# Six channel-wise projections of the state-space layer: eight block products each against seven, with weight sums on GpSimd

## The reference

```python
def ssd_dilated_layer(x, norm_w, w_in, conv_w, conv_b, ...):
    h = rms_norm(x, norm_w)
    proj = jnp.einsum("bsd,df->bsf", h, w_in.astype(h.dtype))
    z, xbc, dt, q, k, v, g = split_cols(proj, EVEN_IN_SIZES)
    xbc = jax.nn.silu(causal_dwconv(xbc, conv_w, conv_b))
    xs, bm, cm = split_cols(xbc, (SSD_D_INNER, SSD_GROUPS * SSD_D_STATE, SSD_GROUPS * SSD_D_STATE))
    ...
    y = ssd_chunked_scan(xs, dt, A, bm..., cm...)
    y = y + d_skip * xs
    y = y.reshape(Bsz, S, SSD_D_INNER) * jax.nn.silu(z)
    ...
```

## Time and profile before

| | |
|---|---|
| median of three runs | 1670.7 us |
| span of the profiled execution | 1666.9 us |
| from that span to the median | 3.8 us |
| TensorE busy | 1564.8 us (94%) |
| VectorE busy | 486.1 us (29%) |
| ScalarE busy | 267.3 us (16%) |
| GpSimd busy | 73.5 us (4%) |
| HBM read | 500.43 MB |

### The profile page before, as it was taken

One profiled execution on the slowest core, in us unless ns is written; L12 is line 12 of the kernel. 1 busy time (PEld: TensorE's weight loads), 2 busy tenths in 40 slices (PEclk: granted clock), 3 DMA queues, 4 the chain that ended last, 5 costly groups with the idle time before them and its releaser, 6 DMA issues. The chain is left out here.

```text
span 1666.9 us, 25063 instructions
## 1 busy us (share of the span) xinstructions
PE 1564.8 (94%) x10674; PEld 1038.9 (62%) x10674; DVE 486.1 (29%) x932; ACT 267.3 (16%) x667; POOL 73.5 (4%) x138
## 2 busy tenths in 40 slices
PE   9999999998989899999999998898999899999998
PEld 8855555555555576465556555554888678758874
DVE  4941000000000313440000000002436897346642
ACT  1020000000000112210000000001132233321331
POOL 0000000000000000000000000000000432001220
PEclk9999999999999899999999999999999999999999
DMA  9689999999999942499999999999233224233420
GB/s 389 268 320 370 429 426 429 427 428 428 428 428 427 398 151 101 181 420 412 428 428 428 429 428 428 428 427 423 109 131 122 102 102 151 102 116 137 152 101 26
DMA packets 38519, 502.52 MB, mean 301 GB/s; under 512 B 4272, under 2 KB 4528, under 8 KB 6064
## 3 DMA queue, kind: packets, MB, share of 16 engines
q1 hardware_dynamic: 37872, 499.40, 72.8%
q0 software_dynamic: 576, 2.10, 0.3%
HBM read 500.43 MB, written 1.05 MB: 301 GB/s over the span
## 5 line engine op out<-in xcount | busy, mean ns | idle before, releaser
L854 PE MATMUL ps<-x_tok,tables_sb 128*128 128x256 f32 x1228 | 305.1, 392 | 0.0
L854 PEld LDWEIGHTS ps<-x_tok,tables_sb 128*128 128x128 f32 x1228 | 220.9, 189 | 102.8 <-issue 77.1
L877 PE MATMUL ps<-ring,arena 128*32 128x256 f32 x3968 | 238.6, 382 | 30.2 <-DMA ring<-in_expert_up 20.5
L877 PEld LDWEIGHTS ps<-ring,arena 128*32 128x32 f32 x3968 | 118.5, 109 | 139.2 <-issue 31.0
L719 PE MATMUL ps<-spare,ring 128*128 128x256 f32 x768 | 169.7, 383 | 0.9 <-DVE spare L2121 0.9
L2357 DVE TENSOR_TENSOR arena<-arena,ps 128x128 f32<-128x128 f32 x64 | 18.4, 288 | 497.0 <-ACT arena L1723 497.0
L719 PEld LDWEIGHTS ps<-spare,ring 128*128 128x128 f32 x768 | 147.3, 192 | 22.3 <-DVE spare L2121 1.2
L940 PE MATMUL ps<-ring,arena 128*32 128x512 f32 x928 | 115.0, 612 | 16.4 <-ACT arena L1718 11.3
L1303 PE MATMUL ps<-ring 128*128 128x256 f32 x480 | 110.5, 383 | 1.4 <-ACT tables_sb L1851 1.3
L751 PE MATMUL ps<-ring,arena 128*128 128x512 f32 x224 | 98.7, 595 | 2.9 <-ACT arena L1841 1.3
L1303 PEld LDWEIGHTS ps<-ring 128*128 128x128 f32 x480 | 89.5, 190 | 18.7 <-issue 6.9
(11 more groups left out here) (299 smaller groups left out, 1396.3 us busy)
## 6 DMA issues: line engine op xcount, KB each, us to landing
ring<-in_expert_up SPq DMA_DIRECT2D x124, 2048.0 KB, 20.4
ring<-in_stream SPq DMA_DIRECT2D x43, 2048.0 KB, 8.2
ring<-in_expert_down SPq DMA_DIRECT2D x42, 2048.0 KB, 24.1
ring<-in_expert_down SPq DMA_DIRECT2D x32, 1024.0 KB, 22.3
arena<-in_expert_up SPq DMA_DIRECT2D x4, 2048.0 KB, 11.2
arena<-in_expert_down SPq DMA_DIRECT2D x2, 2048.0 KB, 12.4
tables_sb<-in_expert_down SPq DMA_DIRECT2D x2, 2048.0 KB, 9.9
spare<-in_expert_down SPq DMA_DIRECT2D x2, 2048.0 KB, 10.2
```

The source lines that it names most:

```text
L854: pe.matmul(ps[:, b, 0:TOK], ident, x[:, 0, 0:TOK], start=True, stop=True, skip_group_check=True)
L877: ins = pe.matmul(ps[q * SLOTS:(q + 1) * SLOTS, 4 + e % 2, 0:TOK] .rearrange("p (g n) -> p g n", g=2), xg[:, 4 * half + k, e * SLOTS:(e + ...
```

## The change

The six channel-wise chunks are made by seven products too.

- PE: `seven_channels` issues for each chunk seven products of two channel blocks by four row blocks, with a 128x128 block of the weight (or of t1 to t4) as the stationary operand and 128 tokens (or a sum of token halves) as the moving one: 56 matmuls, 112 records for a chunk.
- GpSimd: `channel_sums` makes the 24 weight sums of these chunks, 128x1024 each, ahead of the first `rotate`. A chunk's sums wait for its arrival, the first ten also for the last chunks of MOE1, later ones for a free place among the ten.
- ScalarE: `keep` copies three partial results of a chunk out of PSUM. The copies into the padded buffer are gone; the last taps read that buffer, and stand behind the first `keep` of the next chunk. The 16 SiLU are in two groups with a `keep` between, and those of `z` read SBUF.
- VectorE: `channel_corner`, `channel_front` and `channel_crossed` put the quarters together in the padded buffer or in `ss_z`: five additions for a chunk, ahead of the taps. For chunks 4 and 5 they stand in the loop that moves the turned blocks.

The diff, cut to its core:

```diff
-    sevens = [base[stage] + n for stage, which in ((SSD, range(6, 15)), (MOBA, (0, 1, 2, 4, 5, 6)))
+    sevens = [base[stage] + n for stage, which in ((SSD, range(15)), (MOBA, (0, 1, 2, 4, 5, 6)))
               if stage in on for n in which]
+    by_channel = 6 if SSD in on else 0
...
+            if is_channel(g):
+                return 4 + 2 * ((g - base[SSD]) % 2)
...
+        def channel_rows(g):
+            c = g - base[SSD]
+            return ss_pad[:, c % 2, :, 3:3 + TOK] if c < 4 else ss_z[:, 4 * c - 16:4 * c - 12, :]
...
+            def channel_sums():
+                for n in range(4 * by_channel):
+                    c, q = divmod(n, 4)
+                    w = slot8[slot(sevens[c])]
+                    if q == 0:
+                        arrive(pool, sevens[c])
+                    if MOE1 in on and n in (0, 4, 8):
+                        pool.wait_ge(chunk_done, base[SSD] - 2 + n // 4)
+                    if n >= W_SUMS:
+                        c6, q6 = divmod(n - W_SUMS, 4)
+                        if q6 == 3:
+                            pool.wait_ge(chunk_done, sevens[c6] + 1)
+                        else:
+                            pool.wait_ge(sem("product"), 6 * c6 + FREED_AT[q6])
+                    if q in (1, 3):
+                        pool.wait_ge(sem("channel_sums"), n if q == 1 else n - 1)
+                    w11, w12, w21, w22 = (w[:, 4 * a_:4 * a_ + 4, TOK * b_:TOK * b_ + TOK]
+                                          for a_ in range(2) for b_ in range(2))
+                    a_, b_ = ((w12, w11), (w22, w_sum[(n - 1) % W_SUMS]), (w22, w12),
+                              (w21, w_sum[(n - 2) % W_SUMS]))[q]
+                    pool.tensor_tensor(w_sum[n % W_SUMS], a_, b_, ALU.subtract)\
+                        .then_inc(sem("channel_sums"), 1)
...
                 if stage == SSD:
+                    channel_sums()
                     if first < SSD:
                         pool.wait_ge(sem("late_in"), 16 * ((first == CONV) + (first < STICK) + 1))
                     rotate(0, gains)
...
+            def seven_channels(g):
+                c, b, w = seven_no[g], seven_bank(g), slot8[slot(g)]
+                low, high, left, right = slice(0, 4), slice(4, 8), slice(0, TOK), slice(TOK, 512)
+                x1, x2 = xT[:, :, 0:P], xT[:, :, P:TOK]
+                t1, t2, t3, t4 = (w_sum[(4 * c + q) % W_SUMS] for q in range(4))
+                products = (
+                    (b, 0, w[:, low, left], x1[:, low], True),
+                    (b + 1, TOK, t1, x_sum[0], True),
+                    (b, 0, t2, x_sum[1], False),
+                    (b + 1, TOK, w[:, high, right], x_sum[2], False),
+                    (b + 1, 0, t3, x_sum[3], True),
+                    (b, TOK, w[:, high, left], x1[:, high], True),
+                    (b + 1, 0, t4, x2[:, high], False))
+                if c >= 2:
+                    pe.wait_ge(sem("ss_proj"), c - 1)
+                arrive(pe, g)
+                for n, (o_b, at, w_, x_, opens) in enumerate(products):
+                    if 0 < n < 5:
+                        pe.wait_ge(sem("added"), n)
+                    if n in (2, 3, 5):
+                        pe.wait_ge(sem("kept"), 3 * c + (2, 3, 5).index(n) + 1)
+                    if n in (1, 2, 4, 6):
+                        pe.wait_ge(sem("channel_sums"), 4 * c + (1, 2, 4, 6).index(n) + 1)
+                    if n == 6:
+                        pe.wait_ge(sem("added"), added_no(g))
+                    for m in range(2):
+                        for k in range(4):
+                            ins = pe.matmul(ps[:, o_b, at + m * P:at + (m + 1) * P],
+                                            w_[:, k, m * P:(m + 1) * P], x_[:, k, :],
+                                            start=(opens and m == 0 and k == 0), stop=(k == 3),
+                                            skip_group_check=True)
+                    ins.then_inc(chunk_done if n == 6 else sem("product"), 1)
...
-                channels(g, 4)
-                channels(g + 1, 6)
+                seven_channels(g)
+                seven_channels(g + 1)
...
-                for c in (2, 3):
-                    pe.wait_ge(sem("ss_taken"), 8 * (c - 1))
-                    channels(g + c, 4 + 2 * (c % 2))
+                seven_channels(g + 2)
+                seven_channels(g + 3)
...
-                pe.wait_ge(sem("ss_taken"), 8 * 3)
-                channels(g + 4, 4)
+                seven_channels(g + 4)
                 turn_x(0)
                 turn_x(1)
-                pe.wait_ge(sem("ss_taken"), 8 * 4)
-                channels(g + 5, 6)
+                seven_channels(g + 5)
                 turn_x(2)
                 turn_x(3)
...
+                def last_taps(c):
+                    act.wait_ge(sem("ss_proj"), c + 1)
+                    for m in range(4):
+                        k = 4 * c + m
+                        act.activation(xa[:, k, :], ss_pad[:, c % 2, m, 3:3 + TOK], ACT.Identity,
+                                       bias=b[:, k:k + 1], scale=w[:, k, 3:4])\
+                            .then_inc(sem("ss_taken"), 1)
+                def silus(which):
+                    for m in which:
+                        act.wait_ge(sem("ss_conv"), m + 1)
+                        act.activation(xa[:, m, :], xa[:, m, :], ACT.Silu)\
+                            .then_inc(sem("ss_silu"), 1)
+                def gate_silu(c):
+                    act.wait_ge(sem("ss_proj"), 5 + c)
+                    z = ss_z[:, 4 * c:4 * c + 4, :]
+                    act.activation(z, z, ACT.Silu).then_inc(sem("ss_z"), 1)
+                for n in range(3):
+                    keep(g, n)
                 for c in range(4):
                     if c == 2:
                         soft_dt()
-                    done(g + c)
-                    for m in range(4):
-                        src = ps[:, 4 + 2 * (c % 2) + m // 2, (m % 2) * TOK:(m % 2 + 1) * TOK]
-                        k = 4 * c + m
-                        if c >= 2 and m == 0:
-                            act.wait_ge(sem("ss_conv"), 4 * (c - 1))
-                        act.activation(ss_pad[:, c % 2, m, 3:3 + TOK], src, ACT.Copy)\
-                            .then_inc(sem("ss_taken"), 1)
-
-                        act.activation(xa[:, k, :], src, ACT.Identity, bias=b[:, k:k + 1],
-                                       scale=w[:, k, 3:4]).then_inc(sem("ss_taken"), 1)
+                    keep(g + c + 1, 0)
+                    last_taps(c)
+                    keep(g + c + 1, 1)
+                    if c < 3:
+                        keep(g + c + 1, 2)
                 silu_table()
-                for m in range(16):
-                    act.wait_ge(sem("ss_conv"), m + 1)
-                    act.activation(xa[:, m, :], xa[:, m, :], ACT.Silu).then_inc(sem("ss_silu"), 1)
-                for c in range(2):
-                    done(g + 4 + c)
-                    act.activation(ss_z[:, 4 * c:4 * c + 4, :]
-                                   .rearrange("p (b m) t -> p b (m t)", b=2), two_banks(4 + 2 * c),
-                                   ACT.Silu).then_inc(sem("ss_z"), 1)
+                silus(range(8))
+                keep(g + 4, 2)
+                silus(range(8, 16))
+                keep(g + 5, 0)
+                keep(g + 5, 1)
+                gate_silu(0)
+                keep(g + 5, 2)
+                gate_silu(1)
...
+            def channel_corner(g):
+                c, b, o = seven_no[g], seven_bank(g), channel_rows(g)
+                dve.wait_ge(sem("product"), 6 * c + 5)
+                dve.wait_ge(sem("kept"), 3 * c + 2)
+                dve.tensor_tensor(kept[1], kept[1], ps[:, b + 1, 0:TOK], add)\
+                    .then_inc(sem("added"), 1)
+                dve.wait_ge(sem("added"), added_no(g))
+                dve.wait_ge(sem("kept"), 3 * c + 3)
+                dve.tensor_tensor(o[:, 2:4, P:], kept[1].rearrange(halves_of, m=2),
+                                  kept[2].rearrange(halves_of, m=2), add)
+            def channel_front(g):
+                c, b, o = seven_no[g], seven_bank(g), channel_rows(g)
+                dve.wait_ge(sem("product"), 6 * c + 6)
+                dve.tensor_tensor(o[:, 0:2, 0:P], kept[0].rearrange(halves_of, m=2),
+                                  ps[:, b, TOK:].rearrange(halves_of, m=2), add)
+            def channel_crossed(g):
+                c, b, o = seven_no[g], seven_bank(g), channel_rows(g)
+                dve.wait_ge(chunk_done, g + 1)
+                dve.tensor_tensor(o[:, 0:2, P:], kept[2].rearrange(halves_of, m=2),
+                                  ps[:, b + 1, 0:TOK].rearrange(halves_of, m=2), add)
+                dve.tensor_tensor(o[:, 2:4, 0:P], kept[2].rearrange(halves_of, m=2),
+                                  ps[:, b + 1, TOK:].rearrange(halves_of, m=2), add)\
+                    .then_inc(sem("ss_proj"), 1)
+            def channels(g):
```

(12 more changed lines are left out.)

28 lines of the change are left out of this document (18 added, 10 removed).

## The result

The changed kernel takes 1690.5 us (median of four runs, 1689.77 to 1696.61), the kernel before beside it 1670.4: ratio 1.0128, 95% interval 1.0110 to 1.0145, **slower by 20 us** where 20.6 was forecast. The profiled execution is the slowest of the four (1696.6 us, 6.1 over the median; span 1694.8, 27.9 over the span of before), so its terms come out larger than the medians' difference.

A forecast was written before the change was run, and what follows sets the result against it. PE's own time was taken to bound the projections, VectorE's norm chain the start before them. Terms -5.5 + 9.4 + 6.8 + 4.8 + 5.1 = +20.6 gave span 1687.5, plus 3.8 to the median 1691.3 us; range 1680 to 1703 (0.62).

The forecast's parts named there:

- The mechanism and its three places: GpSimd subtractions and VectorE instructions stop each other; PE loses time at the norms, chunk 1's taps and the turned blocks.
- Saving: PE in the six projections: seven products at 1.85 us each, 0.92 less per projection, 5.5 us less in all (0 to 9.3).
- One subtraction: GpSimd, one 128x1024 weight sum: taken as 2.04 us, bounds 2.04 and 2.96.
- terms 3 and 4: Delays from stopped VectorE instructions: the norms ahead of SSD, 9.4 us more, and the taps of chunk 1, 6.8 us more.
- The stops: A VectorE instruction with two SBUF inputs or in a 2-port mode that meets a GpSimd subtraction waits to its end.
- Norms: VectorE's norm chain ahead of SSD: eight instructions stopped by the first ten subtractions, 9.4 us more (0 to 18).
- the rival that only wide ones are stopped: Norm chain: only the four wide VectorE instructions are stopped, costing 5.2 us; time 1687.1 us, chance 0.20.
- Taps of chunk 1: Projection 2: chunk 4's four subtractions begin inside these VectorE taps, so PE's seventh product waits 6.8 us more (0 to 10).
- Turned blocks: Behind projection 5: chunk 6's sums come after chunk 5's additions, so B and C's third product is 4.8 us later (4 to 5.5).
- Clock: PE at its lower clock level after each of three new idle times: 1.7 us each, 5.1 us more (0 to 8).
- The rival in which VectorE goes first: Norms and taps: subtractions wait instead, so those delays vanish; 1666.2 us, or 1667.9 with its clock term, chance 0.10.
- GpSimd did not become the bound: Rival: a sum takes up to 3.2 us, four 12.8, as much as a projection; 1703.1 us, chance 0.08.

The follow-up runs named there:

- halved_sums: The changed kernel with each GpSimd subtraction of 128x1024 made as two of 128x512; 1685.5 us, ratio 1.0095 to the kernel before.
- no_sums: The changed kernel without the 24 GpSimd subtractions, blocks of the chunk read in their place; 1669.9 us, ratio 0.9997 to the kernel before.
- chunk4_sums_later: The changed kernel with GpSimd holding chunk 4's four subtractions until the taps of chunk 2 are done; 1692.2 us, ratio 1.0121 to the kernel before.
- no_sums_chunk6_first: The changed kernel without the 24 subtractions, VectorE making chunk 6's sums ahead of chunk 5's additions; 1663.0 us, ratio 0.9962 to the kernel before.
- before_with_ten: The kernel before, with its own projections, plus the first ten GpSimd subtractions of the changed kernel; 1683.5 us, ratio 1.0077 to the kernel before.
- spaced_sums: The changed kernel with 21 subtractions held to other moments, three made by VectorE, chunk 6's sums first; 1663.5 us, ratio 0.9952 to the kernel before.

## Why the prediction was right, step by step

The mechanism and its three places were as forecast, and so was the time. The closeness of the time is partly luck. In the traces lead and stretch are 25.1 longer where 20.6 was forecast, so the terms were 4.5 too small in sum. The two spans differ by 27.9 and the medians by only 20.1, since the profiled execution of before is some 2 us quicker than its median and that of after 6.1 slower; how much of this lies in lead and stretch is open. The 3.8 us from span to median hold those 2 us too: about 1.8 is what an execution takes over its span.

- **Saving.** Taken 0.92 a projection, measured 1.30, inside its bounds (0 to 1.55). The 1.98 us between L833 and L877 were those of a late wait, not of the shape: a product takes 1.79. The kernel before had a nearer row, which the prediction did not use, 32 records of the same line without a wait, 3.57 us from start to the start of the next line, 1.79 for 16:

```profile
145.10 3.74 PE L833 MATMUL ps<-arena,x_tok 128*128 128x128 f32 x32
```

- **One subtraction.** Taken 2.04, measured 2.34 by itself, mean 2.39 over the 24. This was the mis-sized input of terms 3 and 4. It is not the size alone: in halved_sums a subtraction of 128x512 takes 1.27, where L646 over the same 128x512 takes 1.02 of a pair's 2.04; what makes them differ was not tested. The Trainium skill (GPSIMD Engine Reference, 3.1 Elementwise) gives 4497 ns for 2048 columns, an estimate of 2.25 for 1024; the trace is 4% above it.
- **The stops.** The prediction says of eight L2897 that they got slower one after the other. Singly, the first five take their usual 0.48, and only the last three, beside L646 from 1367.00 on, are stopped (1.27, 1.26 and 0.95). The rule that it draws from them holds all the same.
- **Norms.** Taken 9.4, measured 11.1, shown from both sides: without the ten it goes, with the ten alone it comes. All eight instructions were stopped, the four over one element too (0.37 to 1.82 in place of 0.21), so the rival that only wide ones are stopped falls. By the rule of the Trainium skill (SBUF — State Buffer, Who interferes with whom) a VectorE instruction with two SBUF inputs or in a 2-port mode takes the lock; the trace agrees, with 1.82 us for L2236 and 4.89 for a pair of L2667. That L2237 keeps its 0.21 fits it if one element is not taken in a 2-port mode, which no row shows.
- **Taps of chunk 1.** Taken 6.8, measured 7.68, shown by no_sums and chunk4_sums_later. A further 0.50 in projection 3, from the sums of chunk 5 in the taps of chunk 2, was not foreseen: I had put them behind the taps.
- **Turned blocks.** Taken 4.8, measured 4.60, shown by no_sums_chunk6_first.
- **Clock.** Taken 1.7 behind each of three idle times. Measured against the same instructions at full pace: 1.5, 2.0 and 3.4 (the last from the third product of B to the scan), and 1.6 behind `dt`, where no idle time stands. 8.5 and not 5.1.

The sum of what was measured is -7.8 + 11.1 + 7.7 + 0.5 + 4.6 + 8.5 = 24.6 of the 25.1 in the trace.

The rival in which VectorE goes first, so that the change is not slower, falls: the first ten subtractions took 23.88 in all, only 0.5 over ten times 2.34, though eight VectorE instructions had their turn among them. GpSimd did not become the bound either: at 2.4 us four sums take 9.8, less than a projection.

## What to carry to other kernels

An idle GpSimd is not free: while it runs elementwise work from SBUF, each VectorE instruction with two SBUF inputs, and each that works from SBUF at twice the plain pace, waits for the end of the GpSimd instruction that it meets, whatever its own size (0.21 became up to 1.82 us, 0.44 became 2.4); those that read PSUM did not. Before moving work to it, mark on VectorE's timeline which instructions are of these kinds and are waited for, and release the GpSimd work by semaphores into the stretches between; the subtractions cost 20 us where they fell, and next to nothing with 21 of them placed so and three made by VectorE in its own idle time. Where they can't be placed, shorter GpSimd instructions help a chain with few VectorE instructions (the norms, 11.1 to 5.0 us) but hardly a row of them (the taps, 7.7 to 7.2); in all halving gave back 5.5 of the 20 us.

## What the runs showed that was not expected

- TensorE's clock fell to its lower level behind 3.5 us of records with 16 moving columns, without an idle time: 0.56 granted from 1215.20 to 1218.40. Before the change the same 32 records stood there, and the records of 256 columns behind them lost nothing. In before_with_ten, with the same records of 256 columns, they did: the 16 behind take 5.99 us instead of 3.54, at 0.50. So neither the narrow records alone nor the shape of those around them decides it, and what does stays open; in pieces of eight the narrow records did not bring it about.
- An elementwise instruction over one element per partition took up to 1.82 us beside a subtraction in place of 0.21. What it takes is what is left of the subtraction that it meets.
- GpSimd waits in its turn: 0.18 us beside a tap of 0.48, 1.0 beside a VectorE instruction of 1.2 (spaced_sums).
- Halving the subtractions halved the price on the norms but took only 0.5 of 7.7 us off the taps, where twice as many taps were stopped for half as long.
